# A hybrid attention kernel on one core: the first phase put in another order

## The reference

```
c_act = silu(c)
mod = c_act @ w_ada + b_ada                      # 6 x 1024 numbers
shift_mix, scale_mix, gate_mix, shift_ffn, scale_ffn, gate_ffn = split(mod, 6)
h = rms_norm(x) * (1 + scale_mix) + shift_mix
proj = h @ w_in                                  # 512 x 3072: qa, ka, va, qb, kb, vb
...
kv = rmsnorm(mem, mem_norm) @ w_mem_kv           # in each layer of the second block
```

## Time and profile before

| | |
|---|---|
| median of three runs | 1806.94 us |
| profiled execution | 1808.13 us |
| its span, first to last instruction | 1806.4 us |
| TensorE, matmul | 1772.1 us busy, 98% |
| TensorE, weight load | 1431.0 us, 79% |
| VectorE | 1095.0 us, 61% |
| ScalarE | 732.5 us, 41% |
| GpSimd | 40.6 us, 2% |
| granted TensorE clock, mean | 0.999 |

### The profile page before, as it was taken

One profiled execution on the slowest core, in us unless ns is written; L12 is line 12 of the kernel. 1 busy time (PEld: TensorE's weight loads), 2 busy tenths in 40 slices (PEclk: granted clock), 3 DMA queues, 4 the chain that ended last, 5 costly groups with the idle time before them and its releaser, 6 DMA issues.

```text
span 1806.4 us, 22462 instructions
## 1 busy us (share of the span) xinstructions
PE 1772.1 (98%) x8312; PEld 1431.0 (79%) x8312; DVE 1095.0 (61%) x1601; ACT 732.5 (41%) x1031; POOL 40.6 (2%) x78
## 2 busy tenths in 40 slices
PE   7999899999999999999999999999999999999998
PEld 6887556888888888878888888889766788888887
DVE  6978775655555335775677674245576567777423
ACT  6312664343344223444344443232365434444322
POOL 4110000000000000000000000000000000000000
PEclk9999999999999999999999999999999999999999
DMA  9694112233222323312322222333401232222231
GB/s 355 242 348 140 48 53 95 80 101 106 95 93 87 103 89 96 114 48 93 117 93 93 93 93 92 100 85 109 164 24 47 71 116 93 93 93 93 95 104 70
DMA packets 149081, 195.29 MB, mean 108 GB/s; under 512 B 3646, under 2 KB 133000, under 8 KB 146332
## 3 DMA queue, kind: packets, MB, share of 16 engines
q1 hardware_dynamic: 141272, 155.28, 26.5%
q0 software_dynamic: 7600, 39.13, 5.9%
q10 hardware_dynamic: 148, 0.05, 0.0%
HBM read 189.15 MB, written 5.29 MB: 108 GB/s over the span
## 4 chain that ended last, share of the span: by engine, by line
PE 93%; DVE 4%; ACT 1%; issue 1%; DMA 0%; SPq 0%; ACTq 0%; DVEq 0%
PE bank L809 21%; PE bank L810 21%; PE bank L811 21%; PE bank L872 3%; PE bank L874 2%; PE bank L873 2%; PE bank L1476 2%; PE bank L1475 2%; PE bank L1474 2%; PE bank L956 2%; PE bank L1141 1%; PE bank L1008 1%; PE bank L852 1%; PE bank L853 1%; PE bank L977 1%; PE bank L854 1%
## 5 line engine op out<-in xcount | busy, mean ns | idle before, releaser
L1945 DVE TENSOR_TENSOR w_lo<-w_stage,w_hi 128x2048 fp32r<-128x2048 f32 (+3 forms) x135 | 296.7, 2198 | 435.1 <-ACT w_hi L1502 435.0
L809 PE MATMUL bank<-act_hi,w_hi 128*128 128x512 f32 x1216 | 475.2, 391 | 0.9 <-DVE act_lo L2009 0.6
L811 PE MATMUL bank<-act_hi,w_lo 128*128 128x512 f32 x1216 | 473.3, 389 | 0.0
L810 PE MATMUL bank<-act_lo,w_hi 128*128 128x512 f32 x1216 | 473.2, 389 | 0.0
L1502 ACT ACTIVATE w_hi<-w_stage 128x2048 fp32r<-128x2048 f32 (+3 forms) x137 | 251.7, 1837 | 461.6 <-PE bank L811 333.9
L809 PEld LDWEIGHTS bank<-act_hi,w_hi 128*128 128x128 f32 x1216 | 228.2, 188 | 50.5 <-DVE act_lo L2009 2.1
L811 PEld LDWEIGHTS bank<-act_hi,w_lo 128*128 128x128 f32 x1216 | 228.2, 188 | 47.5
L810 PEld LDWEIGHTS bank<-act_lo,w_hi 128*128 128x128 f32 x1216 | 228.3, 188 | 47.4 <-issue 0.5
L809 PE MATMUL bank<-mid_hi,w_hi 128*128 128x512 f32 x352 | 136.9, 389 | 0.0
L810 PE MATMUL bank<-mid_lo,w_hi 128*128 128x512 f32 x352 | 136.9, 389 | 0.0
L811 PE MATMUL bank<-mid_hi,w_lo 128*128 128x512 f32 x352 | 136.9, 389 | 0.0
(11 more groups left out here) (412 smaller groups left out, 2631.7 us busy)
## 6 DMA issues: line engine op xcount, KB each, us to landing
ada_stage<-in_w_ada POOLq DMA_DIRECT2D x24, 1024.0 KB, 7.1
w_stage<-in_w_up SPq DMA_DIRECT2D x22, 1024.0 KB, 5.0
w_stage<-in_a_ffn_in SPq DMA_DIRECT2D x22, 1024.0 KB, 5.1
w_stage<-in_b_ffn_in SPq DMA_DIRECT2D x22, 1024.0 KB, 5.1
w_stage<-in_w_in SPq DMA_DIRECT2D x10, 1024.0 KB, 7.2
w_stage<-in_b_ffn_out SPq DMA_DIRECT2D x10, 1024.0 KB, 5.1
w_stage<-in_w_down SPq DMA_DIRECT2D x8, 1024.0 KB, 5.2
w_stage<-in_a_ffn_out SPq DMA_DIRECT2D x8, 1024.0 KB, 5.2
```

The costliest lines, as they stand in the source:

```text
L809: pe.matmul(dst, wh, mh, start=start and k == 0, stop=False)
L810: pe.matmul(dst, wh, ml, start=False, stop=False)
L811: last = pe.matmul(dst, wl, mh, start=False, stop=stop and k == nk - 1)
L1945: dve.tensor_tensor(w_lo[slot][:, 0:n], raw[:, 0:n], w_hi[slot][:, 0:n].bitcast(FP32), ALU.subtract).then_inc(w_ready, 1)
```

## The change

All is in the first 60 us of the program.

1. The memory products stand between the memory turns. Product pair k (both output tiles, one feature tile) follows turn pair k + 4; the last four pairs follow the last turn. The first waits for the weights.
2. x turns go to banks 6, 7, 0 and 1, since the memory products hold banks 4 and 5. ScalarE waits for its last `x_norm` copy before it scales.
3. The scale's sums come from eight products of `ada_acc` with a column of ones, each giving 128 sums in one column of bank 2. VectorE adds 1 and the bias straight from the bank; the reduction goes.
4. VectorE's subtraction for chunk 0 is made in two halves, `w_half` after features 0 to 3 and `w_ready` after 4 to 7; the second half stands before the fourth `act_lo`.
5. Chunk 0 is done feature by feature, both output tiles for each.

```
+            def xn_bank(k):
+                return bank[(6, 7, 0, 1)[k % 4]]
...
+            def mem_product(k):
+                pe.wait_ge(tr_saved, TR0["mem"] + k + 1)
+                if k == 0:
+                    pe.wait_ge(w_mem_loaded[0], 16)
+                for m in range(2):
+                    mem_half(0, m, [k])
+            MEM_LAG = 4
             pe.wait_ge(mem_diag, 2)
+            for k in range(KT):
+                turn_mem(k)
+                if k >= MEM_LAG:
+                    mem_product(k - MEM_LAG)
+            for k in range(KT - MEM_LAG, KT):
+                mem_product(k)
...
-            pe.wait_ge(xn_saved, KT)
-            pe.wait_ge(w_mem_loaded[0], 16)
-            mem_half(0, 0, range(4))
             pe.wait_ge(consts_set, 14)
             pe.wait_ge(ada_added, 8)
-            ada_sum(range(8, 16), 2)
-            mem_half(0, 0, range(4, KT))
-            mem_half(0, 1)
+            for j in range(8):
+                last = pe.matmul(bank[2][:, j:j + 1], ada_acc[:, P * (8 + j):P * (9 + j)], one_col,
+                                 start=True, stop=True)
+            last.then_inc(mod_summed, 1)
+            pe.wait_ge(xn_saved, KT)
...
+            pe.wait_ge(w_half, 1)
+            for k in range(KT):
+                if k == KT // 2:
+                    pe.wait_ge(w_ready, 1)
+                for m in range(2):
+                    part(0, 0, m, [k], act, tile_wait=normed("w_in_scaled") if m == 0 else None,
+                         start=k == 0, stop=k == KT - 1)
...
             split_at(0)
+            act.wait_ge(xn_saved, KT)
             act.wait_ge(scaled, SPLIT0["w_in_scaled"] + 8)
...
             dve.wait_ge(mod_summed, 1)
-            dve.tensor_reduce(out=mod[:, 8:16], in_=banks[:, 2:4, :].rearrange("p b (c n) -> p (b c) n", n=P),
-                              axis=AXIS.X, op=ALU.add).then_inc(mod_added, 1)
-            dve.wait_ge(mod_added, 1)
-            dve.scalar_tensor_tensor(out=mod[:, 8:16], in0=mod[:, 8:16], scalar=1.0, in1=vec[:, P + 8:P + 16],
+            dve.scalar_tensor_tensor(out=mod[:, 8:16], in0=bank[2][:, 0:8], scalar=1.0, in1=vec[:, P + 8:P + 16],
                                      op0=ALU.add, op1=ALU.add).then_inc(scaled, 8)
-            split_w(0, 0)
+            def first_split(half):
+                dve.wait_ge(w_hi_done, 1)
+                part = slice(1024 * half, 1024 * half + 1024)
+                dve.tensor_tensor(w_lo[0][:, part], w_stage[0][:, part], w_hi[0][:, part].bitcast(FP32),
+                                  ALU.subtract).then_inc(w_ready if half else w_half, 1)
+            first_split(0)
...
             for t in range(KT):
+                if t == 3:
+                    first_split(1)
                 low_scaled(t)
```

More of the change, by code:

```diff
@@ L340, in program @@
         w_hi_done = sem("w_hi_done")
-        w_ready = sem("w_ready")
+        w_ready, w_half = sem("w_ready"), sem("w_half")
         tile0_done = sem("tile0_done")
@@ L1113, in scaled_turn, with turn_mem @@
                                  stop=True)
-            pe.wait_ge(mem_diag, 2)
-            for k in range(KT):
+            def turn_mem(k):
                 n = TR0["mem"] + k
@@ L1144, in mem_half @@
                     last.then_inc(mem_done if m else mem_tile, 1)
+            def mem_product(k):
[5 more added lines that the diff above has]
+            MEM_LAG = 4
+            pe.wait_ge(mem_diag, 2)
+            for k in range(KT):
[4 more added lines that the diff above has]
+                mem_product(k)
             pe.wait_ge(x_diag, NT)
             for k in range(KT):
-                if k == 2:
-                    pe.wait_ge(tr_saved, TR0["mem"] + KT)
                 if k >= 4:
@@ L1153, in _ @@
                 for t in range(NT):
-                    last = scaled_turn(bank[4 + k % 4], x_tok[:, t, P * k:P * (k + 1)], t)
+                    last = scaled_turn(xn_bank(k), x_tok[:, t, P * k:P * (k + 1)], t)
                 last.then_inc(xn_turned, 1)
-            pe.wait_ge(xn_saved, KT)
-            pe.wait_ge(w_mem_loaded[0], 16)
-            mem_half(0, 0, range(4))
             pe.wait_ge(consts_set, 14)
             pe.wait_ge(ada_added, 8)
-            ada_sum(range(8, 16), 2)
-            mem_half(0, 0, range(4, KT))
-            mem_half(0, 1)
+            for j in range(8):
[3 more added lines that the diff above has]
+            pe.wait_ge(xn_saved, KT)
             def shift_sum():
@@ L1167, in shift_sum @@
                 ada_sum(range(8), 0)
+            pe.wait_ge(w_half, 1)
[5 more added lines that the diff above has]
+                         start=k == 0, stop=k == KT - 1)
             for j in range(4):
-                chunk(C0["qk_a"] + j, j % 2, KT, CHUNK_COLS, act, g=G0["qk_a"] + j, gslot=j % 2,
-                      tile_wait=normed(("w_in_scaled", "", "w_in", "")[j]) if j % 2 == 0 else None,
+                if j:
+                    chunk(C0["qk_a"] + j, j % 2, KT, CHUNK_COLS, act, g=G0["qk_a"] + j, gslot=j % 2,
+                      tile_wait=normed("w_in") if j == 2 else None,
                       chunk_wait=(scaled, SPLIT0["w_in_scaled"] + 8) if j == 1 else None,
@@ L1727, in _ @@
                 act.wait_ge(xn_turned, k + 1)
-                act.activation(x_norm[:, k, :], bank[4 + k % 4][:, :], ACT.Copy).then_inc(xn_saved, 1)
+                act.activation(x_norm[:, k, :], xn_bank(k)[:, :], ACT.Copy).then_inc(xn_saved, 1)
             def save_x(tiles):
@@ L2111, in mod_columns @@
                     .then_inc(mod_added, 1)
-                dve.wait_ge(mod_added, n + 1)
+                dve.wait_ge(mod_added, n)
                 dve.tensor_scalar(mod[:, 8 * scale:8 * scale + 8], mod[:, 8 * scale:8 * scale + 8],
@@ L2328, in shift_columns @@
                                   axis=AXIS.X, op=ALU.add).then_inc(mod_added, 1)
-                dve.wait_ge(mod_added, 2)
+                dve.wait_ge(mod_added, 1)
                 dve.tensor_tensor(mod[:, 0:8], mod[:, 0:8], vec[:, P:P + 8], ALU.add).then_inc(mod_ready, 1)
             for t in range(KT):
+                if t == 3:
+                    first_split(1)
                 low_scaled(t)
```

## The result

The changed kernel takes 1813.33 us (median of seven runs, 1811.01 to 1814.06) against 1807.91 us for the kernel before, run beside it (seven runs, 1806.60 to 1809.48). The ratio is 1.0031, 95% interval 1.0022 to 1.0040: slower by 5.6 us by the ratio (5.4 by the medians), 4 to 7 us by the interval. The forecast was +4.3 us, a ratio of 1.0024. In time it was 1811.2 us, and of the 2.1 us that this is short, 1.0 is the kernel before, whose median over seven runs is 1807.91 and not 1806.94.

What follows compares the result with a forecast made beforehand. TensorE, busy 98% of the span, bounds the kernel, VectorE's block second. That block starts 4.9 us late, act_hi 4.3, carried to the end: 1806.94 becomes 1811.2 us, range 1808.4 to 1814.0, chance 0.50.

Steps and rivals of the forecast that it cites:

- The wait for the weights: After memory turn 4, TensorE stands from 15.4 us until the memory's key weights land at 18.8, about 3.4 us.
- From the landing to the end of the x turns: From 18.8 us, 15.4 us of TensorE work plus 2.5 for a slow start; x turns end at 36.7, against 29.2.
- The sentence that doubted the clock column: Early transposes: half pace read as 1.2 GHz, later pace as 2.4, though the granted clock shows 1.00 in every stretch.
- The path behind the x turns: Before chunk 0: w_hi ends 2.4 us after the last x_norm copy starts, hiding the ones; act_lo 0 at 41.0.
- by VectorE and no longer by TensorE: At the shift, VectorE's block, 4.9 us late, releases ScalarE's act_hi at 65.0 us against 60.73.
- rival A: TensorE falls back in the hole before chunk 0, running slow about 5 us: +5.9 us, 1812.8 us; chance 0.22.
- The sum: Chunk 0 starts 3.4 us late, VectorE's block 4.9, act_hi 4.3; VectorE carries +4.3 us to chunk 3 and the end.
- Rival B: The slow stretch after the weights land is short or absent: +1.8 us, 1808.7 us; chance 0.19.
- Rival C: Weights there when turn 4 ends and TensorE fast at once; x turns end at 30.4: -2.0 us, 1804.9 us; chance 0.06.
- next to nothing to win: Even the best case gains 0.11%, as w_hi and half subtraction behind the x turns, 4.3 us, are no longer hidden.
- Rival D: The delay does not reach the end because some later wait takes it up; chance 0.03.

Runs made afterwards that it cites:

- e2: Kernel before with only the memory products moved among the memory turns and the change's other banks for x: 1816.24 us, ratio 1.0044.
- e3: Changed kernel with twelve unread identity products between the products with ones and chunk 0: 1811.68 us, ratio 1.0023.
- e8: Changed kernel with unread identity products before and among the memory turns and twelve before chunk 0: 1811.38 us, ratio 1.0020.
- e4: Changed kernel whose sixteen memory products read the memory tile as weights and wait for no load: 1809.54 us, ratio 1.0012.
- e1: Changed kernel with the sixteen memory products put back behind the x turns: 1808.98 us, ratio 1.0006.
- e9: Changed kernel with the load of the memory's key weights issued ahead of the load of x: 1811.11 us, ratio 1.0019.
- e6: Kernel before with halves, both tiles per feature, other x banks; products behind x turns, six before the transposes, no wait for last x_norm copy: 1807.97 us, ratio 1.0002.
- e5: Kernel before with unread identity products ahead of the first transposes and after the memory turn pairs: 1807.08 us, ratio 0.9999.

## Why the prediction was right

It named the sign, and its size lies in the interval. One step failed, the fourth below. By its steps:

- **The wait for the weights.** Right in kind: the first memory product waited for the load. In the profiled run it landed at 16.6, the sum had 18.8. In e2, e3 and e8, with the same order, it was 18.1 to 18.4. e4 took the wait away, and with it and the slow pace behind it went 3.4 to 3.8 us.
- **From the landing to the end of the x turns.** Forecast 15.4 us of work and 2.5 us for the slow part, 17.9; measured 16.74 to 34.84, 18.1 us. That a TensorE that had stood starts slow was argued from one stretch; here it did, and against e8 the cost is 2.5 us. This is as the Trainium skill has it ("TensorE: Matmul & The Clock Gate", section "What's actually happening": the throttled state is the default). In e2's profile the cost is 2.8 us, in e3's, where TensorE started fast and fell later, 1.7, so 2.5 isn't the same in every execution. The sentence that doubted the clock column stands as well: in the changed kernel the column reads 1.00 from 17 to 19 us, where the products come at half pace, and 0.59 around 41 us, where they do too. I take it that it knows no level ahead of the first change; that is inferred. e1 fits: there the column falls at 19.4 and reads 0.50 while the x turns are slow, as it did not in the profile of before (rows in the last section).
- **The path behind the x turns.** w_hi ended 2.4 us after the last copy started (37.27), the block began at 37.30, act_lo 0 came 2.0 us later; forecast 2.4 and 1.9. The ones took 1.84 us and were hidden by w_hi with 0.5 us to spare.
- **The step that failed: "by VectorE and no longer by TensorE".** TensorE fell to the lower level in the hole before chunk 0, as rival A said, for six products and not for 5 us. It cost 1.2 us on TensorE, of which 0.5 reached the end, since VectorE's shift was nearly as late. So what happened is the forecast plus a small A: A had its mechanism right and its price, 1.6 us over the forecast, too high for this run. e2 and e9 had the longer fall that A assumed, 0.43 us apart for eleven products in e9; of the 2.2 us that it cost TensorE in e9 about 1.3 reached chunk 3.
- **The sum.** At chunk 3 +3.0 us in the profile, where +4.3 was forecast. The landing was 2.2 us earlier than the sum has it, and A's 0.5 us came on top. With a landing at 18.4 to 18.8 in place of 16.6 it would be 4.8 to 5.2 us, an estimate; the medians differ by 5.4 us. That the forecast came within 1.1 us of them, with a fall that it didn't have, is in part luck.
- **Rival B** is out for this kernel: the slow stretch was there, from the landing to about 21.5 us.
- **Rival C** was half right: with the weights there TensorE is fast at once, and chunk 3 started 0.4 us earlier than before in e4's profile; its price was 2.0 us. The x turns ended 0.8 us later than it had them, and the fall before chunk 0 took 0.7 more. The claim that even then there is next to nothing to win held: -2.0 us was the bound, and over the runs it is slower by 0.12%.
- **Rival D** is out: chunk 3 and the span moved alike, 3.0 and 2.9 us. In no profile of e1 to e9 either was more than 0.2 us made up behind chunk 3, against the kernel before.

Open: how far the landing varies from run to run of one kernel, since only profiled runs show it, and how often the kernel before has its x turns slow.

## What to carry to other kernels

Work that is moved ahead in an engine's list takes its waits along, and everything behind it stands with it: look up when its operands have landed in full before moving it. Ask also what the work was covering where it stood; here 7 us of products hid the rounding and subtracting on two other engines, which take 4.5 us from the last x_norm copy to act_lo 0 in the changed kernel, and in their new place they hid none of it. A hole can cost more than its length: behind one of 2.8 us TensorE lost another 1.2 us, because six products came at half pace, and behind one of 2.2 us in e9 another 2.2, with eleven.

## What was not expected of the hardware

The pace at which TensorE starts work after a sparse stretch differed between executions of the same instructions: x turns at 1.66 us per feature tile in the profile of before and 0.89 in that of e6, with the same memory turns ahead. In e1 the last memory turns were fast already (four loads in 0.52 us at 16.8, where eight took 1.78 before); then TensorE stood for 1.68 us, fell, and made the x turns slowly until 26 us. The windows of the changed kernel (first row) and of e1:

```profile
17.00:19.00 2.00, 2.00 (x6) 1.64 (x6) 0.50 (x2) 0.00 (x0) 1.13 (x3) 1.00 1.04 414
...
20.00:25.00 5.00, 5.00 (x24) 5.00 (x25) 4.72 (x5) 1.19 (x2) 0.00 (x0) 0.50 0.98 383
```

Single falls also came far behind the first phase, in waits of the attention loops, where the code is the same in all kernels: in e3, e4 and e5 between 200 and 220 us, in e2, e6 and e9 between 275 and 290 us (this is e6, granted clock 0.66), and in none of the other five profiles.

```profile
275.00:280.00 5.00, 5.00 (x13) 3.36 (x14) 2.03 (x3) 2.08 (x4) 0.00 (x0) 0.66 0.00 0
```

Each of the six takes 1.7 us of TensorE's time by the granted clock. What they cost can be read from the table, as what the span gained beyond chunk 3, both against the kernel before: 0.5 to 0.7 us in e3, e4 and e5, 1.6 us in e2, e6 and e9, and between -0.1 and 0 in the four others. So a fall near 280 us is paid nearly whole and one near 205 us by a third. Time and the granted clock of the whole run go together as well: of 73 runs of the kernel before, timed beside e1 to e9, those at 0.999 took 1806.8 us on average (22 runs), at 0.998 1807.8 us (34) and at 0.997 1809.1 us (17). These 2.3 us are about half of the spread of 1806.1 to 1810.9 us. What starts such a fall was not tested.
